# Second mixer of a two-block fp32 network: query sums side by side, key norms over the value tiles, gate tiles in halves, weight splits at projection steps

## The reference

```python
def gqa_mixer(h, hc, w_in, w_out, qk_g, cos, sin, with_ctx_out):
    def project(t):
        p = t @ w_in
        q, k, v, z = jnp.split(p, [GQ_Q_WIDTH, GQ_Q_WIDTH + GQ_KV_WIDTH, GQ_Q_WIDTH + 2 * GQ_KV_WIDTH], axis=-1)
        q = rms_norm(q.reshape(B, L, GQ_HEADS, GQ_HEAD_DIM), qk_g[0])
        k = rms_norm(k.reshape(B, L, GQ_KV_HEADS, GQ_HEAD_DIM), qk_g[1])
        ...
    q = apply_rope(q, cos, sin)
    k = apply_rope(k, cos, sin)
    k_all = jnp.concatenate([k, kc], axis=1)
    v_all = jnp.concatenate([v, vc], axis=1)
    o = sweep_attention(q, k_all, v_all)
    return (o * jax.nn.silu(z)) @ w_out
```

## Time and profile before

| | |
|---|---|
| runs | 1536.14, 1543.64, 1540.22 us; median 1540.22 |
| the profiled execution | own time 1536.65 us, span 1534.9 us |
| granted clock of TensorE, mean | 0.897 |
| busy: PE, DVE, ACT, POOL | 1300.8 (85%), 819.3 (53%), 600.1 (39%), 54.3 (4%) us |
| matmul records | 8530 |
| tiles split | 272 casts, mean 1038 ns; 272 `w_lo`, mean 1213 ns |
| stretches of the second mixer | query tiles 1284.6 to 1345.4; key tiles to 1360; key norms to 1374; value tiles to 1388.6; attention to 1485.6; `w_out1` to 1518; end 1534.9 |

### The profile page before, as it was taken

One profiled execution on the slowest core, in us unless ns is written; L12 is line 12 of the kernel. 1 busy time (PEld: TensorE's weight loads), 2 busy tenths in 40 slices (PEclk: granted clock), 3 DMA queues, 4 the chain that ended last, 5 costly groups with the idle time before them and its releaser, 6 DMA issues.

```text
span 1534.9 us, 22640 instructions
## 1 busy us (share of the span) xinstructions
PE 1300.8 (85%) x8530; PEld 1139.9 (74%) x8530; DVE 819.3 (53%) x1611; ACT 600.1 (39%) x1077; POOL 54.3 (4%) x58
## 2 busy tenths in 40 slices
PE   3899998997966898999989899987878997677776
PEld 3898887887964897988979788963445887666556
DVE  3565544558646755555664444347763445553443
ACT  3774345342210343443433356434431344433332
POOL 0000000002012000000000000000000000110000
PEclk9899998988977999999999799978667998779878
DMA  5254343432211352488747422210000332211100
GB/s 229 97 178 152 126 150 110 137 111 83 97 69 42 125 182 87 168 289 293 289 168 261 175 83 96 101 51 0 1 1 28 110 125 95 70 45 52 56 1 28
DMA packets 47963, 175.01 MB, mean 114 GB/s; under 512 B 5328, under 2 KB 5968, under 8 KB 47216
## 3 DMA queue, kind: packets, MB, share of 16 engines
q1 hardware_dynamic: 47232, 169.77, 31.4%
q0 software_dynamic: 624, 3.80, 0.7%
HBM read 172.50 MB, written 1.05 MB: 113 GB/s over the span
## 4 chain that ended last, share of the span: by engine, by line
PE 64%; issue 15%; DVE 10%; ACT 4%; POOL 0%; ACTq 0%; DVEq 0%; POOLq 0%
PE lin L1021 15%; PE lin L1022 14%; PE lin L1023 14%; PE o_bank L1132 3%; PE sum_bank L1083 3%; PE lin L1035 2%; PE lin L1036 2%; PE lin L1037 2%; ACT w_hi L1236 2%; DVE w_lo L1423 1%; PE sum_bank L1095 1%; PE score L1112 1%; PE score L1155 1%; PE score L1053 1%; PE pt_bank L1122 1%
## 5 line engine op out<-in xcount | busy, mean ns | idle before, releaser
L1423 DVE TENSOR_TENSOR w_lo<-w_raw,w_hi 128x1024 fp32r<-128x1024 f32 (+1 forms) x272 | 329.2, 1213 | 368.2 <-ACT w_hi L1236 304.6
L1236 ACT CAST w_hi<-w_raw 128x1024 fp32r<-128x1024 f32 (+1 forms) x272 | 279.0, 1038 | 160.9 <-PE lin L1023 128.7
L1021 PE MATMUL lin<-XH,w_hi 128*128 128x256 f32 x448 | 134.6, 300 | 1.1 <-DVE w_lo L1423 0.7
L1022 PE MATMUL lin<-XL,w_hi 128*128 128x256 f32 x448 | 131.6, 294 | 0.0
L1023 PE MATMUL lin<-XH,w_lo 128*128 128x256 f32 x448 | 131.4, 293 | 0.0
L1021 PE MATMUL lin<-NH,w_hi 128*128 128x256 f32 x416 | 120.3, 289 | 0.0
L1022 PE MATMUL lin<-NL,w_hi 128*128 128x256 f32 x416 | 117.6, 283 | 0.0
L1023 PE MATMUL lin<-NH,w_lo 128*128 128x256 f32 x416 | 117.5, 283 | 0.0
L1083 PEld LDWEIGHTS sum_bank<-ones,sqr 128*128 128x128 f32 x400 | 63.5, 235 | 53.2 <-ACT sqr L1270 49.3
L1083 PE MATMUL sum_bank<-ones,sqr 128*128 128x2 f32 x400 | 63.6, 273 | 41.5 <-ACT sqr L1270 37.2
L1021 PEld LDWEIGHTS lin<-XH,w_hi 128*128 128x128 f32 x448 | 91.2, 204 | 5.1 <-issue 5.0
(11 more groups left out here) (348 smaller groups left out, 3271.1 us busy)
## 6 DMA issues: line engine op xcount, KB each, us to landing
w_raw<-in_ada SPq DMA_DIRECT2D x48, 512.0 KB, 5.8
w_raw<-in_w_out SPq DMA_DIRECT2D x32, 512.0 KB, 3.2
w_raw<-in_gate SPq DMA_DIRECT2D x22, 512.0 KB, 6.0
w_raw<-in_up SPq DMA_DIRECT2D x22, 512.0 KB, 3.7
w_raw<-in_ffn_out SPq DMA_DIRECT2D x16, 512.0 KB, 3.8
w_raw<-in_q SPq DMA_DIRECT2D x16, 512.0 KB, 3.7
w_raw<-in_z SPq DMA_DIRECT2D x16, 512.0 KB, 3.2
w_raw<-in_k SPq DMA_DIRECT2D x10, 512.0 KB, 3.2
```

The costliest lines, as they stand in the source:

```text
L1021: nc.tensor.matmul(bank[:, 0:W], wh, moving(H, kk), start=first, stop=False)
L1022: nc.tensor.matmul(bank[:, 0:W], wh, moving(L, kk), start=False, stop=False)
L1236: scal.copy(w_hi[:, i % HL, 0:n], raw[:, tile["i"] % RAW, 0:n]).then_inc(w_hi_ready, 1)
L1423: vec.tensor_sub(w_lo[:, i % HL, 0:n], raw[:, tile["i"] % RAW, 0:n], w_hi[:, i % HL, 0:n].bitcast(F32)).then_inc(w_lo_ready, 1)
```

## The change

It changes the list of steps in the second mixer, and the rule by which splits are placed in the whole program. The parts:

1. **Query sums side by side.** The sums of the eight query tiles go to columns 0, 4, 8 ... of one bank (`pt_bank`), and only the first waits for the bank. The eight `ms` and powers become one of each, on 8 x 2 values, behind the first key tile.
2. **Key norms over the value tiles.** The sums of key head 0 stand behind `k_3` tile 1, those of key head 1 behind the first half of `v_3`, followed by the spreading, head norm and rope of head 0; those of head 1 follow the second half. The head norm waits for its own key tile, a head's scores for the rope of its own key head.
3. **Gate tiles in two halves.** A new step `begin` issues the first 12 matmuls of a `z_3` tile at the first half of a head; the other 12, with the evacuation, follow at the second.
4. **Splits at projection steps.** At every step that is not `lin` the look-ahead is one less. The splits then stand at the `lin` steps, ahead of the evacuation. This holds for all stages of the program.
5. **Output in four pieces.** Four DMAs of 256 KB, each issued when its two `post` steps are done.

```diff
@@ second mixer
         q_norms = [new_norm(P, T) for _ in range(GQ_HEADS)]
+        for t, N in enumerate(q_norms):
+            N["bank"], N["col"] = pt_bank, 4 * t
...
             steps.append(("sqmm", late["sq"]))
-            rt_step(late["N"])
             if late["t"] is not None:
                 rope_step(QB[:, late["t"], :], 64, tab2[:, 2, :], tab2[:, 3, :], late["g"])
+            else:
+                rt_step(late["N"])
...
             lin_step("k_3", t, DT, True, W3, 2 * T, ("qk3", KB, ("qk_g", 1), k_norms[t]))
             finish(late)
+            if t == 0:
+                steps.append(("rt", {"N": q_norms[-1], "n": q_norms[0]["n"], "tts": T // P, "many": GQ_HEADS}))
             late = {"sq": lin_sq[0], "N": k_norms[t], "t": None}
-        finish(late)
-        for t in range(GQ_KV):
+
+        def k_ready(t):
             bc_step(k_norms[t])
...
         for part in range(2):
             lin_step("v_3", 0, DT, False, W3, 2 * T, ("tok", VB, 0, None), "split", part)
-        roped_3 = n_rope[0]
+            if part == 0:
+                finish(late)
+            k_ready(part)
...
             if part == 0:
                 lin_step("z_3", t, DT, True, W3x, T, ("act", ZB))
+                held.append(steps.pop())
+                steps.append(("begin", held[0][1]))
+            else:
+                steps.append(held.pop())
@@ SP
-            sp.wait_ge(res_ready, last_res)
-            sp.dma_start(out_dram, X2[:, :, :]).then_inc(stored, 16)
-            sp.wait_ge(stored, 16)
+            for k in range(0, DT, 2):
+                sp.wait_ge(res_ready, last_res - DT + k + 2)
+                sp.dma_start(out_dram[:, k:k + 2, :], X2[:, k:k + 2, :]).then_inc(stored, 16)
+            sp.wait_ge(stored, 16 * DT // 2)
@@ sums of squares, PE
-                if s["k"] == 0:
+                c0 = s["N"].get("col", 0)
+                if s["k"] == 0 and not c0:
...
@@ ACT and DVE, the walk over the steps
                 else:
-                    split(pos + LOOK, stream)
+                    split(pos + LOOK - 1, stream)
```

More of the change, by code:

```diff
@@ L782, in finish @@
             steps.append(("sqmm", late["sq"]))
-            rt_step(late["N"])
             if late["t"] is not None:
                 rope_step(QB[:, late["t"], :], 64, tab2[:, 2, :], tab2[:, 3, :], late["g"])
-        def q_tile(t):
+            else:
+                rt_step(late["N"])
+        for t in range(8):
             lin_step("q_3", t, DT, True, W3x, T, ("qk3", QB, ("qk_g", 0), q_norms[t]))
             finish(late)
-            return {"sq": lin_sq[0], "N": q_norms[t], "g": n_lin[0] - 1, "t": t}
-        for t in range(8):
-            late = q_tile(t)
+            late = {"sq": lin_sq[0], "g": n_lin[0] - 1, "t": t}
             own_sums()
@@ L825, in head_gq @@
             return made
-        fills_3 = [0]
+        fills_3, held = [0], []
         def fill_gq():
@@ L866, in program @@
                 done_groups += 1
-        seen_rt_q = max(n["rti"] for n in q_norms + k_norms) + 1
+        seen_rt_q = q_norms[-1]["rti"] + 1
         w_out_pos = max(s["pos"] for k, s in steps if k == "lin" and s["stage"] == "w_out")
@@ L1011, in products @@
                         continue
-                    for k in range(tile["n"]):
+                    for k in range(tile["n"]) if ks is None else ks:
                         wh = w_hi[:, slot, k * P:(k + 1) * P]
@@ L1023, in products @@
                         last = nc.tensor.matmul(bank[:, 0:W], wl, moving(H, kk), start=False, stop=final)
-                    last.then_inc(w_used, 1)
+                    if ks is None or ks[-1] == DT - 1:
+                        last.then_inc(w_used, 1)
                 if s["feat"]:
@@ L1082, in sq @@
                     src = sqr2[:, s["m"] % 4, tt * P:(tt + 1) * P] if own else sqr[:, s["m"] % 2, tt * P:(tt + 1) * P]
-                    last = nc.tensor.matmul(bank[:, 2 * tt:2 * tt + 2], src, ones[:, 0:2], start=(s["k"] == 0 and tt == 0),
+                    last = nc.tensor.matmul(bank[:, c0 + 2 * tt:c0 + 2 * tt + 2], src, ones[:, 0:2], start=(s["k"] == 0 and tt == 0),
                                             stop=(s["k"] == s["K"] - 1 and tt == s["tts"] - 1))
@@ L1523, in rt_ @@
                 dve.wait_ge(sq2_used if s["N"]["own"] else sq_used, s["N"]["m"])
+                if "many" in s:
+                    q = s["many"]
+                    sums = s["N"]["bank"][:, 0:2 * w * q].rearrange("p (q t two) -> p q t two", t=w, two=2)[:, :, :, 0]
+                    vec.tensor_scalar(ms[:, s["n"]:s["n"] + q, 0:w], sums, s["N"]["inv"], EPS, ALU.mult, ALU.add)\
+                        .then_inc(ms_ready, 1)
+                    return
                 sums = s["N"]["bank"][:, 0:2 * w].rearrange("p (t two) -> p t two", two=2)[:, :, 0]
@@ L1615, in headn @@
                 if s["gain"] is None:
-                    after_lin(dve, stage_last["k_3"])
+                    after_lin(dve, s["g"])
                     vec.tensor_mul(s["dst"], s["dst"], r).then_inc(res_ready, 1)
```

24 lines of the change are left out of this document (18 added, 6 removed).

## The result

The changed kernel takes 1446.02 us (median of 4 runs, 1445.13 to 1446.86) against 1540.72 before, beside each other: a ratio of 0.9388, 95% interval 0.9364 to 0.9412. The direction was right and the size was not: 94.7 us by the medians and 90.5 by the profiled executions (1536.65 to 1446.14), where 64.9 were forecast, and the time lies 6 us under the range.

What follows compares the result with a forecast made beforehand. TensorE bounds the kernel, idle behind short DVE results in wrongly ordered queues. From 1536.65 us, terms -9.5 - 9.6 - 6.4 - 9.0 - 9.5 - 19.5 - 1.4 = -64.9 give 1472; range 1452 to 1496.

Steps and rivals of the forecast that it cites:

- Splits at projection steps: Whole program: moved splits no longer hold up short DVE results; start -9.5, first attention -9.6, middle -6.4 us.
- the fourth stretch: Cross attention with its two residual projections; the forecast gave it 0.
- Query sums: Eight query tiles: without the wait for `ms`, 53 in place of 60.8 us; with the key sums' 1.5, together -9.0.
- a sign against me: Query stage: still longer than 57 us would show the forecast wrong.
- Key norms over the values: End of key tiles to end of value tiles: norm of head 0 under `v_3`'s second half, 28.6 to about 19, -9.5 us.
- Gate halves: Second mixer's heads: 12 gate matmuls at each half cover the wait for `probs`; 8.6 us a head, -19.5 in sum.
- Output in four pieces: End of kernel: the last 256 KB lands in 2.5 us where 1 MB took 3.9, -1.4 us.
- More clock: Query stage to end, plus first attention: closed gaps keep TensorE at 2.4 GHz, 14 us more, 1458 in all; chance 0.17.
- The head loop keeps half its time: Second mixer's heads: TensorE waits for `wideT` instead of `probs`; 15 of the 19.5 us stay, 1487; chance 0.10.
- Only the second mixer: Outside it, results are late for another reason; the first three terms' 25.5 us stay, 1497; chance 0.08.
- names only: Whole kernel: the waits only change their names, 1536 us; chance 0.04.
- Slower: Stages with attention or ropes: splits come too late, 1.2 us at about 96 tiles costs 115, 1587; chance 0.04.

## Why the prediction was wrong, point by point

**What bounds the kernel.** Right: TensorE idle behind short results in wrongly ordered queues. The reading stopped one step short. The row with `w_lo` says [5.21 <-issue], and that of the earlier trace rows says 12.84 for `w_hi`. I read 1.2 us of `w_lo`, where the row showed DVE idle for several us until a cast was done that itself stood behind an evacuation. At the start I did follow this chain and came near; elsewhere I did not look for it.

**Splits at projection steps.** This is the step that failed: the term priced a moved `w_lo` at its own 1.2 us, took in no clock, and put the splits at nothing in the recurrence, in the fourth stretch and in the whole second mixer. Outside the second mixer: forecast -25.5, measured -41.9 by putting the old rule back, and -43.7 by the traces, 18 of the 26 us by which the sum was short. `w_out0` was 11.6, not 5.2: its two waits, and 5.1 of busy time that went with the clock. The recurrence was left out altogether and gave 9.8, as the waits for `qk` shrank. The fourth stretch was left out and took 6.7 back: I had checked that `w_lo` left the way of short results, and not what it now stands in the way of. Inside the second mixer I gave the splits nothing; alone they win 33 of the 46.8 that went there, where the forecast had 39.4 from the other parts.

**Query sums.** Forecast -9.0; beside the new splits worth nothing that can be measured, and at most the 3.5 of the list's parts with the old rule. The wait went and the stage did not follow: the eight tiles went from 60.8 to 55.4, and stand at 55.9 with the splits alone. My 6.65 us a tile was a guess between two bounds; the stage lies at 6.9 (55.4 in all, under the 57 that would have been a sign against me), so the guess was near and its cause was wrong.

**Key norms over the values.** Forecast -9.5, measured -7.5 by undoing it (8.6 in its own stretch); the right size. The first scores start 16.9 us after the second key tile's last matmul, where about 19 were forecast.

**Gate halves.** Mechanism right and its credit wrong: the wait for `probs` went (20.8 to 2.0) and the heads fell by 25.0 where I had 19.5. But 22.4 come without the halves, whose own part is 2 to 3. The head takes 8.41 us against 8.6 forecast. That the term was 5.5 short in spite of this has to do with the heads before the change: three behind the first took 12.4, 12.0 and 11.8, which is 3.8 more than the 10.8 each that I had read off one.

**Output in four pieces.** As forecast: the last stretch by 1.6 (1.4), the pieces 2.4 us each (2.5). The +6 that I had estimated from the Trainium skill ("DMA: Bandwidth & Descriptors", rules for kernel authors) for four transfers paid one after another did not come; in the trace the first three lie beside `post` steps.

**The rivals.** *More clock* was the nearest, at 1458 with 0.17, and it was half right: stages that lost their waits lost busy time too (-38.3 in all, against some 52 of idle time). But filled waits alone gave 5 us in all, though they took the clock of their two stretches to 0.97 and 0.96; most of what it gives comes together with the removed waits, and it should have been in each term. By its page's rule alone (the Trainium skill, "TensorE: Matmul & The Clock Gate", what's actually happening) the query stage would have gone to 1.0. It stayed at 0.77, with TensorE busy for 49.05 of 58.8; `w_out0`, where its idle time went to 0, did go to 1.00. *The head loop keeps half its time*: the wait for `wideT` is 0.97 a head and not more. *Only the second mixer*, *names only*: no. *Slower*: not here, but real with a look-ahead of two.

## What to carry to other kernels

In a queue that runs in order, ask of each instruction what it stands behind, and follow that back until it ends in the engine that is the bound: work done ahead of time (a cast, a split of weights) belongs ahead of an evacuation that waits for that engine, unless the evacuation's own result is what the engine waits for. The length of a moved instruction is not its price, and the idle time ahead of it in its row is only an upper bound: 5.21 us in a head, of which the head at full clock got back 2.2 (10.8 to 8.6 with the splits alone). The wait of TensorE behind it (2.35 there) came nearest. Where a gap is closed, look for what the same matmuls take at the higher clock too. When several edits aim at one wait, only one of them will earn it; run each alone as well as undoing each, since undoing one of two that do the same shows next to nothing.

## What the runs showed that I had not expected

Extra matmuls that nobody reads, placed in TensorE's waits, made the kernel faster by 0.35% (0.2 to 0.5), with the granted clock of two stretches up by 0.05 and 0.07. A wait of 5.4 us in front of TensorE, in a stage whose chain goes through DVE and ACT too, cost 0.5. And one tile of look-ahead decides between 1446 and 1573 us, with waits for `w_lo` of 9 us at three and 114 at two.
